# Tiles paired behind two norms, fillers of attention one place sooner, ranks ahead of the second choice, and the first expert split during the mixing

## The reference

```
h  = x + rms_norm(concat(ssd(p), rwkv7(p)) @ w_out)        with p = rms_norm(x) @ w_in
h  = h + rms_norm((silu(gate) * val) @ ffn_down)           [gate, val] = conv3(rms_norm(h) @ ffn_up)
h1 = rms_norm(h) * (1 + sc1) + sh1
y0 = gmlp(h1), y1 = gated_linear_attention(h1), y2 = top-128-key attention(h1), 4 heads
x  = h + gt1 * (sum_n sigmoid(gates_n) * (y_n @ w_branch_n)) @ w_out2
x  = x + gt2 * moe(rms_norm(x) * (1 + sc2) + sh2)          4 groups of 4 experts, 1 group, 2 experts a token
```

## Time and profile before

| | us |
|---|---|
| median of 3 runs | 1792.78 (1789.63 to 1801.59) |
| the profiled execution | 1786.85 |
| its span, first to last instruction | 1785.0 |
| TensorE matmul busy | 1678.0 (94%) |
| VectorE busy | 1202.3 (67%) |
| ScalarE busy | 481.5 (27%) |
| GpSimd busy | 676.7 (38%) |
| mean granted TensorE clock | 0.980 |

### The profile page before, as it was taken

How to read it: one execution, slowest core, us unless ns; L and a number is a source line. 1 busy time by engine, 2 the same in 40 slices (tenths; PEclk the granted TensorE clock), 3 DMA queues, 4 the chain that set the end, 5 groups by cost and what they waited for, 6 DMA issues and landing times.

```text
span 1785.0 us, 29266 instructions
## 1 busy us (share of the span) xinstructions
PE 1678.0 (94%) x11954; PEld 1299.6 (73%) x11954; DVE 1202.3 (67%) x1601; ACT 481.5 (27%) x739; POOL 676.7 (38%) x382
## 2 busy tenths in 40 slices
PE   7999988899699999999699999999998997999998
PEld 6887667777487777777478788778777866666665
DVE  6959786656588888888675179387554616666674
ACT  4122344422210011001231122221231005545452
POOL 4665000023166666666346534336344641000000
PEclk9999999999899999999899999999999998999999
DMA  6222531131242222222222212113212245788884
GB/s 246 95 94 95 178 108 50 51 120 49 77 172 95 94 94 94 79 88 91 94 72 95 95 48 72 48 48 115 88 51 71 94 189 201 293 353 328 342 336 161
DMA packets 34069, 230.52 MB, mean 129 GB/s; under 512 B 4132, under 2 KB 4388, under 8 KB 8232
## 3 DMA queue, kind: packets, MB, share of 16 engines
q1 hardware_dynamic: 30240, 214.48, 33.1%
q10 hardware_dynamic: 2136, 10.24, 1.5%
q0 software_dynamic: 1584, 4.21, 0.7%
HBM read 220.98 MB, written 9.50 MB: 129 GB/s over the span
## 4 chain that ended last, share of the span: by engine, by line
PE 80%; DVE 12%; ACT 3%; DMA 3%; issue 2%; DVEq 0%; POOL 0%; SPq 0%; POOLq 0%; ACTq 0%
PE psum L421 79%; DVE arena L1715 3%; DVE arena L1709 2%; DMA arena<-units 2%; PE psum L425 2%; ACT arena L1305 1%; DVE arena L1712 1%; DVE expert_lo L1709 1%; DMA normed<-units 1%; ACT expert_hi L1305 1%; DVE residual L1709 0%; DVE arena L2344 0%; DVE smalls L2341 0%; DVE tiny L1723 0%; DVE yb_lo L1709 0%
## 5 line engine op out<-in xcount | busy, mean ns | idle before, releaser
L1305 ACT ACTIVATE arena<-psum 128x512 f32<-128x512 f32 (+3 forms) x298 | 150.7, 521 | 816.4 <-PE psum L421 751.7
L421 PE MATMUL psum<-arena 64*64 64x64 f32 (+6 forms) x2852 | 218.8, 261 | 24.3 <-DVE arena L1709 12.8
L421 PE MATMUL psum<-normed_hi,w_in_hi 128*128 128x512 f32 x504 | 202.5, 402 | 7.4 <-DVE in_lo L1709 4.8
L421 PEld LDWEIGHTS psum<-arena 64*64 64x64 f32 (+4 forms) x2852 | 147.5, 146 | 80.4 <-issue 48.7
L421 PE MATMUL psum<-normed_hi,w_in_lo 128*128 128x512 f32 x504 | 200.6, 398 | 0.0
L421 PE MATMUL psum<-in_lo,w_in_hi 128*128 128x512 f32 x504 | 199.0, 395 | 0.0
L1715 DVE SCALAR_TENSOR_TENSOR arena<-arena,fixed_data 128x512 f32<-128x512 f32 x138 | 184.6, 1339 | 13.5 <-DVE arena L1712 0.2
L1709 DVE TENSOR_TENSOR arena<-arena,psum 128x512 f32<-128x512 f32 (+2 forms) x200 | 110.5, 588 | 110.4 <-PE psum L421 64.5
L2591 POOL TENSOR_TENSOR w_ff_lo<-weight_ring,w_ff_hi 128x1024 fp32r<-128x1024 f32 x66 | 167.1, 2532 | 5.5
L2591 POOL TENSOR_TENSOR w_in_lo<-weight_ring,w_in_hi 128x1024 fp32r<-128x1024 f32 x63 | 159.2, 2528 | 5.2
L2589 POOL TENSOR_SCALAR w_in_hi<-weight_ring 128x1024 fp32r<-128x1024 f32 x63 | 72.4, 1149 | 203.6 <-PE psum L421 192.9
(11 more groups left out here) (251 smaller groups left out, 3426.9 us busy)
## 6 DMA issues: line engine op xcount, KB each, us to landing
weight_ring<-units SPq DMA_DIRECT2D x124, 1024.0 KB, 4.9
arena<-units SPq DMA_DIRECT2D x55, 1024.0 KB, 7.6
normed<-units SPq DMA_DIRECT2D x20, 1024.0 KB, 7.9
slots<-arena ACTq DMA_DIRECT2D x7, 516.0 KB, 8.8
arena<-slots SPq DMA_DIRECT2D x7, 516.0 KB, 5.7
fixed_data<-fixed ACTq DMA_DIRECT2D x1, 2944.0 KB, 9.6
arena<-x SPq DMA_DIRECT2D x4, 512.0 KB, 5.9
arena<-bias_rows ACTq DMA_DIRECT2D x2, 896.0 KB, 4.4
```

The lines of the kernel that those rows point to most:

```text
L421: return nc.tensor.matmul(o, l, r, start=start, stop=stop)
L1305: return nc.scalar.activation(o, i, func, **kw)
```

## The change

1. `pair_of_tiles`: behind both norms the first two tiles are computed together, step by step, as the input tiles come. So that the next chunk can be split meanwhile, the very first chunk of `w_ff` and of `w_in2` lies in a place of its own (`WeightsAfter`), and the third chunk no longer waits for `split_used`. POOL splits chunk 0 before the last tile ahead of the norm is through, chunk 1 right after it, and chunk 2 once the residual is updated (`split_after`).
2. The sums of the second half of each norm use bank 0 instead of bank 4.
3. DVE's last round of the FFN loop is written out: `accumulate` of 4 tiles, `finish_gate`, then the other 4.
4. Attention: `masked(0)` and `gate_branch(0, 6)` move ahead of the last round of the top keys, `probabilities(0)` into it; `masked(1)` behind the first of the three masks. TensorE does part 1 of branch 1 ahead of the loop, so each filler comes one place sooner; in the place of the last one, and behind `values(15)`, stand the first two gate tiles of branch 2 (`early_gate`). The gate products of branch 1 move from t = 2, 3 to t = 1, 2. The first three chunks of branch 2 have places of their own (`WeightsApart`), and POOL splits them from `logits` 15 on.
5. Expert 0 is split during `mix2` (ACT behind squares 2 and 3, DVE behind tiles 3 and 4). A root of one element behind square 6 loads ACT's table for the next root.
6. Routing: the second choice moves behind `hot`. ACT waits for `rows_placed` ahead of the experts. Many buffers change place.

```diff
+            def pair_of_tiles(weights, rhs, outs, ready):
+                w = [[part_.rearrange("p (k c) -> p k c", k=KT) for part_ in take(weights)] for _ in range(2)]
+                o = [open_(what, k, b) for what, k, b in outs]
+                for k in range(KT):
+                    pe.wait_ge(sem(ready), k + 1)
+                    for i, (hi, lo) in enumerate(w):
+                        begun = mm(o[i], hi[:, k, :], rhs.hi(k), k == 0, False)
+                        if k == i * (KT - 1):
+                            begun.then_inc(sem("split_used"), 1)
+                        mm(o[i], lo[:, k, :], rhs.hi(k), False, False)
+                        last = mm(o[i], hi[:, k, :], rhs.lo(k), False, k == KT - 1)
...
-            sums("sum_pre_ffn", sq8, "sq_pre_ffn")
+            sums("sum_pre_ffn", sq8, "sq_pre_ffn", 0)
...
+                if ready:
+                    pair_of_tiles(w_ff, in_ff, [(kind + "_up", (phase, sub, i), i) for i in range(2)], ready)
...
-            project("p2", 1, w_in2, in2, MISC, ready="h_ready")
+            pair_of_tiles(w_in2, in2, [("p2", MISC + i, i) for i in range(2)], "h_ready")
...
+            def early_gate(m, bank):
+                q = chunk[0] + 1 + m
+                pe.wait_ge(sem("split_ready"), q + 1)
+                close(tile_of(w_br[2].slot(q), KT, P, 0, in2, open_(("gates", 2), m, bank), True), ("gates", 2), m)
...
             branch_part(1, 0, (1, 2, 3, 7) * 2)
+            branch_part(1, 1, (1, 2, 3, 7) * 2)
             for i, (hh, t) in enumerate(pairs):
                 attend(hh, t)
                 if i:
                     values(*pairs[i - 1])
                 if i + 2 < len(pairs):
                     logits(*pairs[i + 2])
-                if i + 1 < len(pairs):
-                    branch_part(1, i + 1, (1, 2, 3, 7) * 2)
-            values(*pairs[-1])
+                    branch_part(1, i + 2, (1, 2, 3, 7) * 2)
+                elif i + 1 < len(pairs):
+                    early_gate(0, 1)
...
-            branch(2)
+            values(*pairs[-1])
+            early_gate(1, 2)
+            for i in range(2):
+                branch_part(2, i, (0, 4))
+            chunk[0] += 2
+            for i in [4, 5, 2 + 4, 3 + 4] + list(range(8, 16)):
+                branch_part(2, i, (7, 5, 1, 2, 3, 6, 0, 4))
...
+            for k in range(KT):
+                emptied(act, "mix2", k)
+                f(A(SQ2 + k % 4 * T), res[:, k, :], ACT.Square).then_inc(sem("sq_2"), 1)
+                if k in (2, 3):
+                    expert_hi(0, k - 2)
+                if k == KT - 2:
+                    f(tiny[:, 0:1], C("ones", b=1), ACT.Sqrt)
...
+            it = times - 1
+            conv_gate((it, 1), "loop", 1, it)
+            accumulate("ffn", "loop", 0, it)
+            finish_gate((it, 1), 1)
+            conv_gate((it, 2), "loop", 0, it)
+            accumulate("ffn", "loop", 1, it, range(4))
+            finish_gate((it, 2), 0)
+            accumulate("ffn", "loop", 1, it, range(4, KT))
...
+                if r == 15:
+                    probabilities(0)
...
+                if r == 14:
+                    masked(0)
+                    gate_branch(0, KT - 2)
...
-                if t >= 2:
-                    gate_branch(1, i // 4 * 2 + t - 2)
+                if 1 <= t < 3:
+                    gate_branch(1, i // 4 * 2 + t - 1)
...
+            def split_after(weights, n, what, k, n_updated):
+                split_unit(weights, 0, None, 1)
+                filled(pool, what, k)
+                split_unit(weights, 0, None, 2, 1)
+                unit[0] += 2
+                pool.wait_ge(sem("x_updated"), n_updated)
+                split_unit(weights, 1, None, 1, 0)
+                split_unit(weights, 1, None, 2, 1)
+                split_rest(weights, 2, n)
...
+            filled(pool, ("logits", 3), 3)
+            split_unit(w_br[2], 0)
+            split_unit(w_br[2], 1, None, 1, 0)
             filled(pool, "dsa_y", 3)
-            split_units(w_br[2], 6 + 4)
+            split_unit(w_br[2], 1, None, 2, 1)
+            split_rest(w_br[2], 2, 6 + 4)
```

More of the change, by code:

```diff
@@ L177, in slot, with __init__ @@
                 return self.hi[:, c], self.lo[:, c]
+        class WeightsAfter(Weights):
+            def __init__(self, name, off, chunk, hi_off, lo_off):
+                super().__init__(name, off)
+                self.chunk = chunk
+                self.first = [part(name + n, o, CHUNK) for n, o in (("_first_hi", hi_off), ("_first_lo", lo_off))]
+            def slot(self, q):
+                if q == self.chunk:
+                    hi, lo = self.first
+                    return hi[:, :], lo[:, :]
+                return super().slot(q)
+        class WeightsApart(Weights):
+            def __init__(self, name, hi_off, lo_off, chunk, first_hi_off, third_off):
+                self.hi, self.lo = part(name + "_hi", hi_off, 2 * CHUNK), part(name + "_lo", lo_off, 2 * CHUNK)
+                self.chunk, self.first_hi = chunk, part(name + "_first_hi", first_hi_off, 2 * CHUNK)
+                self.third = part(name + "_third", third_off, 2 * CHUNK)
+            def slot(self, q):
+                hi, lo = super().slot(q)
+                i = q - self.chunk
+                if i == 2:
+                    return self.third[:, 0:CHUNK], self.third[:, CHUNK:2 * CHUNK]
+                return self.first_hi[:, i * CHUNK:(i + 1) * CHUNK] if 0 <= i < 2 else hi, lo
         class Tiles:
@@ L922, in up @@
             def up(kind, phase, sub, it=None, ready=None):
-                for i in range(4):
+                if ready:
+                    pair_of_tiles(w_ff, in_ff, [(kind + "_up", (phase, sub, i), i) for i in range(2)], ready)
+                for i in range(2 if ready else 0, 4):
                     w = take(w_ff, it, 12)
@@ L966, in _ @@
                       "bias_row", i)
-            sums("sum_1", sq8b, "sq_1")
+            sums("sum_1", sq8b, "sq_1", 0)
             spread_rs("sum_1")
             last_rows(1, 1)
-            project("p2", 1, w_in2, in2, MISC, ready="h_ready")
-            emptied(pe, "p2", MISC)
-            for m in range(2):
-                close(mm(open_("forget", m, 4 + m), M("gate2")[:, m * P:(m + 1) * P], p2(MISC)), "forget", m)
-            project("p2", 4, w_in2, in2)
+            pair_of_tiles(w_in2, in2, [("p2", MISC + i, i) for i in range(2)], "h_ready")
+            for t in range(8):
+                w = take(w_in2)
+                close(tile_of(w, KT, P, 0, in2, open_("p2", t, t % 4), True), "p2", t)
+                if t == 0:
+                    emptied(pe, "p2", MISC)
+                    for m in range(2):
+                        close(mm(open_("forget", m, 4 + m), M("gate2")[:, m * P:(m + 1) * P], p2(MISC)), "forget", m)
             last_columns(1)
@@ L1683, in rows_hi @@
                     f(xt_hi[xt_of(b)][:, c], xt_raw[xt_of(b)][:, c], ACT.Copy).then_inc(sem("rows_hi"), 1)
-            for s in range(2):
-                expert_hi(s, 0)
-                expert_hi(s, 1)
+            expert_hi(1, 0)
+            expert_hi(1, 1)
             rows_hi(0)
+            act.wait_ge(sem("rows_placed"), 16 * NT)
             for s in range(NX):
@@ L2133, in finish_gate, with accumulate @@
                     split(acts, 2 * sub + i, "ffn_act_ready")
-            def accumulate(kind, phase, sub, it=None):
-                for m in range(KT):
+            def accumulate(kind, phase, sub, it=None, tiles=range(KT)):
+                for m in tiles:
                     k = (phase, sub, m)
@@ L2145, in _ @@
             times = (NF - 1) // 2
-            with dve.Fori(0, times) as it:
+            with dve.Fori(0, times - 1) as it:
                 ch.enter(it, 24)
@@ L2373, in _ @@
                 link(ts(ma[t], sc[t], -3e38, -1e30, ALU.is_gt, ALU.mult))
-            masked(0)
-            masked(1)
-            probabilities(0)
-            for m in range(KT - 2, KT):
-                gate_branch(0, m)
+                if t == 1:
+                    masked(1)
+            gate_branch(0, KT - 1)
             for i in range(16):
@@ L2574, in unit_loaded, with split_unit @@
                 pool.wait_ge(sem(f"weights{u % RING}_loaded"), v if it is None else it * (16 * per // RING) + v)
-            def split_unit(weights, i, it=None, halves=2):
+            def split_unit(weights, i, it=None, halves=2, first=0):
                 u, q = unit[0] + i, chunk[0] + 2 * i
                 unit_loaded(u, it, 2)
-                for c in range(halves):
-                    if i:
+                for c in range(first, halves):
+                    if i > 1 or i == 1 and (c or weights not in (w_ff, w_in2, w_br[2])):
                         pool.wait_ge(sem("split_used"), q + c if it is None else it * 4 + (q + c))
```

164 lines of the change are left out of this document (83 added, 81 removed).

## The result

The changed kernel takes 1770.36 us (median of 4, 1768.58 to 1778.21) against 1792.48 (median of 4): ratio 0.9875, 95% interval 0.984 to 0.991, 22.1 us or 1.2% faster. Forecast were 1767 us, 1757 to 1782, and faster by over 1% with 0.80; the interval's upper end, 0.9% faster, lies a little within that 1%.

What follows compares the result with a forecast made beforehand. TensorE was taken to bound the kernel, so only filling its gaps or lifting the clock beside them helps. Gains of 26.6 us less 1.6 gave 25.0, and 1767 us was forecast against the 1792.78 median, range 1757 to 1782.

Steps and rivals of the forecast that it cites:

- First norm: First norm up to DVE's hold in the first FFN step: POOL's silence, bank 0 and paired tiles gain 3.4 us (2.5 to 4.3).
- The pair: First two tiles behind each norm computed together: saves 1.2 to 2.9 us in the first; second from 14.4 to 11.3 or 13.0.
- The bank: Both norms: sums in bank 0 needn't wait for the spread root in bank 4 to be read, saving 1.4 us each.
- End of the FFN: Last FFN step: finish_gate ahead of the last four accumulations starts the last down 1.9 us earlier; with clock 3.2 (1.0 to 4.5).
- Second norm: Second norm, same edits: 0.6 us for POOL, 1.4 for the bank, plus the pair; gain 4.3 (3.4 to 5.2).
- Attention: Attention to the mixing: fillers and early gates gain 5.6 us at the start and 6.0 at the end, less 1.3 for cadence.
- the cadence: Attention loop: gate merges ahead of the widest masks, DVE meeting POOL; 1.3 us lost (0 to 7).
- Routing: Routing ahead of expert 0: second choice off the chain, table loaded beforehand, less half clock; gain 4.1 us (2.7 to 5.7).
- the table: Routing: ACT's table loaded beforehand lets the root start 0.9 us earlier; 2.3 by the Trainium skill's drain.
- Expert 0 in the mixing: Mixing: ACT's roundings and DVE's subtractions for expert 0 placed there lose 0.3 us (0 to 2); POOL in time, narrowly.
- would be late next: Routing: expert 0's subtraction, 4.49 us from 1491.14, must move too, else it would end at 1495.6 and be late.
- the rivals: Whole kernel: partly given back 1781.5 us (0.14), clock never falls 1760.7 (0.09), nothing moves 1784 (0.05), slower 1814 (0.04).

Runs made afterwards that it cites:

- table_ahead: The changed kernel with one more one-element Silu on ACT ahead of its new wait for the placed rows; median 1766.22 us, ratio 0.9838 to the kernel before.

## Why the prediction was right, point by point

**First norm (3.4 forecast, 3.7 and 3.0 by pairs of profiles).** POOL's silence 0.87 (0.8 forecast). The pair 2.7, or about 1 with a fall of the clock (1.2 to 2.9 forecast, with just that reason). The bank 1.04 instead of 1.4 (the sums end 0.7 us behind the last square, not 0.46), and 0.9 of it is lost against a block that keeps the clock (4 of 6), as the spread behind paced sums is at half clock in every profile; that term was near nothing. The pair, at the upper part of its range, made up for it in the first profile, and in the second the kernel before had lost the same 0.9: the stage's 3.4 is in part luck. DVE passed on what TensorE gained, the hold stayed 1.57.

**End of the FFN (3.2; 3.05).** 1.9 for the start, measured 1.9 by undoing it; 1.3 for the clock, measured 0.8 to 1.1. The gap of 2.5 that should stay is 2.38.

**Second norm (4.3; 3.4).** The pair 2.7 (1.4 to 3.1 forecast) and POOL 0.63 (0.6); the bank's 1.4 was the mis-sized term: 1.13 less 0.91 for the half-clock spread, 0.2. The sum fell on the low end.

**Attention (10.3 in all; 9.8).** Its parts were less right than their sum. Undoing the early gates costs 6.1 to 7.0 (6.0), with POOL's stall of 0.84 (0 to 1). At the start the gap did not go wholly: 1.37 stay ahead of the long filler, whose bank the last merge of branch 0 frees, on DVE behind the masks; so 3.0 and not 4.37. The clock's 1.4 did come: the 5 us behind the gap read 1.00, where the kernel before has 2.9 us at 0.50. So the start gave about 4.4 of 5.6. Of the 1.3 for the cadence nothing is seen: between 1250.85 and 1337.87 TensorE has no gap of 0.15 us or more. The two errors cancel, which is luck. The parts add up to more than 9.8, since undoing an edit is not adding it: against the kernel before, the gap at branch 2 shrank by 3.4 with 2.1 of clock behind it, and at the mixing's first tiles TensorE waits 0.84 and 0.40 where it waited 0.81; 4.4 + 5.5 - 0.4 = 9.5.

**Routing (4.1; 3.6).** The second choice 1.83 (1.85); the table 0.48 (0.9), as the load already lay beside DVE's two steps; the clock 1.3 (1.4), by 64 matmuls in 9.01 instead of 10.31 us, and 2.9 in the three profiles where they took 7.4. The Trainium skill's drain (ScalarE: Activation LUTs, What ACT_TABLE_LOAD costs) would have made the table term 2.3; the run without the early Sqrt lost 0.5, so no row here shows it on the path.

**Expert 0 in the mixing (-0.3; 0.0).** POOL was held 2.9 us and had 20.1 to spare. What the Trainium skill says of a VectorE operation with two SBUF inputs beside GpSimd (SBUF — State Buffer, Who interferes with whom) the trace agrees with: POOL's operations beside the two subtractions took 2.79 and 2.29 us instead of 1.05. As a price it came to nothing. The edit itself gained 0.4 to 0.8: the step that the subtraction "would be late next" was right in sign only.

**The step that was missing.** The prediction gave the expert phase nothing, and it lost 3.2 us (286.5, the mean of ten profiles, against 283.3, the mean of two). It names no cost for the wait that the change adds on ACT for the placed rows, behind which the Silu's table load is queued: 1.3 us, shown by `table_ahead`. For the other 2 no cause is shown: one kernel's own profiles differ by 2.4 to 4.6 there, so two profiles against ten can neither show nor rule out that the change causes them. The waits behind the turns sum to 4.8 on average in the ten (3.2 to 7.0) and to 2.6 and 4.5 in the two. Whether the earlier start of the experts makes the weights later by a little stays open; the same order of DVE's queue holds TensorE in both kernels.

So the time was forecast 3.4 us too low in the median (1767 against 1770.4). Stage by stage the gain was forecast 5.0 us too high (25.0 against 20.0): 3.2 of it is the expert phase, 0.9 the second norm, 0.5 each attention and routing. Of the signs named beforehand, the paired tiles were full 10.9 us after their start (within 13) and the gap at the end of the FFN is 2.38; three came out otherwise: a gap of 1.37 stays at the start of attention, the sums end 0.7 us behind the last square, and the first rows come 2.3 us sooner, not 2.7. None of the rivals came: DVE did not bound the FFN loop (the hold is 1.57 in every profile), and what was given back was given back elsewhere.

## What to carry to other kernels

When a wait is added in an engine's program, look at what else stands behind it, a table load too: it will start with the wait's end, and an idle engine ahead of it is no cover. In a queue that runs in order, put the work whose inputs are there ahead of the work that waits for a transfer; here TensorE had no wait of 0.25 us or more left behind the turns of expert 0, in the one profile taken, where the two kernels have 2.6 to 7.0 us of them. And cut two traces at the same events before subtracting them: an unchanged stage differed by 14 us between executions.

## What the runs showed of the hardware

The clock fell within unchanged work, and differently in each execution: the window from 180 to 225 us reads 0.70 to 1.00 over the 14 profiles (0.70 in the second of the changed kernel, 0.85, 0.92 and 1.00 above). Nor does a gap decide it alone: behind the same gap of 2.4 us at the end of the FFN (first row the changed kernel, second the one without pairs) the next 8 us were

```profile
859.27:867.27 8.00, 8.00 (x28) 6.43 (x29) 4.35 (x7) 1.90 (x3) 6.84 (x4) 0.79 0.36 120
```

```profile
861.74:869.74 8.00, 8.00 (x35) 6.65 (x36) 5.09 (x8) 2.72 (x5) 6.90 (x4) 1.00 0.36 115
```

28 matmuls in the one and 35 in the other; from the hold to the root behind the FFN the one without pairs took 332.05 us, the ten others with this gap 333.7 to 333.8. And 8 us of small matmuls with pauses of 0.5 to 0.8 us between groups of eight left the clock at half behind them in 22 of 22 cases, a solid block of 64 behind a longer silence in 2 of 6.
